# Scaling the samples by a diagonal, left halves first, and a last stage over 128 partitions: one hybrid layer step on one core

## The reference, cut to what matters

```python
def trunk(x, ...):
    h = rmsnorm(x, norm1_g)
    u_s5, x_rg, g_rg, q, k, v, o, gi, gf = split(h @ w_in)
    y1 = s5_mixer(u_s5, ...)      # step = exp(log_step); mag = exp(lr*step); cos, sin(li*step); complex scan
    y2 = rglru_mixer(x_rg, ...)   # causal conv of 4, two sigmoids, scan
    y3 = mlstm_mixer(q, k, v, gi, gf, o, ...)
    x = x + concat(y1, y2, y3) @ w_out
    x = x + moe(rmsnorm(x, norm2_g), ...)   # 32 experts: w1 1024x2048, w2 1024x1024
    return rmsnorm(x, final_norm_g)         # x / sqrt(mean(x*x) + eps) * g
```

## Time and profile before

| | us |
|---|---|
| median of 3 runs (lowest, highest) | 1098.44 (1097.82, 1098.92) |
| the profiled execution | 1098.81 |
| its span, first to last instruction | 1097.0 |
| PE busy | 1036.5 (94%) |
| DVE busy | 316.1 (29%) |
| ACT busy | 197.9 (18%) |
| POOL busy | 95.3 (9%) |
| moved | 429.45 MB, 391 GB/s over the span |
| chain that ended last | PE 55%, DMA 36%, DVE 5%, ACT 2% |

### The profile page before, as it was taken

How to read it: one execution, slowest core, us unless ns; L and a number is a source line. 1 busy time by engine, 2 the same in 40 slices (tenths; PEclk the granted TensorE clock), 3 DMA queues, 4 the chain that set the end, 5 groups by cost and what they waited for, 6 DMA issues and landing times.

```text
span 1097.0 us, 13183 instructions
## 1 busy us (share of the span) xinstructions
PE 1036.5 (94%) x5134; PEld 435.2 (40%) x5134; DVE 316.1 (29%) x640; ACT 197.9 (18%) x418; POOL 95.3 (9%) x177
## 2 busy tenths in 40 slices
PE   8999999999999999899889989999899989998997
PEld 5767745334333433343333323333324233433322
DVE  5889456312131212121202112121212121212023
ACT  5543615401110201011000201020102010100002
POOL 6899000000000000000000000000000000000000
PEclk9999999999999999999999999999999999999999
DMA  7533799999999999999999999999999999999995
GB/s 223 194 114 77 260 370 406 427 426 431 430 433 430 430 431 431 431 431 431 434 431 431 431 431 431 431 431 434 431 430 431 431 431 431 431 433 431 424 426 239
DMA packets 62051, 429.45 MB, mean 391 GB/s; under 512 B 12022, under 2 KB 25054, under 8 KB 33342
## 3 DMA queue, kind: packets, MB, share of 16 engines
q1 hardware_dynamic: 60868, 428.16, 93.5%
q10 hardware_dynamic: 1146, 0.79, 0.2%
HBM read 424.68 MB, written 3.67 MB: 390 GB/s over the span
## 4 chain that ended last, share of the span: by engine, by line
PE 55%; DMA 36%; DVE 5%; ACT 2%; issue 1%; SPq 1%; ACTq 0%; DVEq 0%
DMA ring_a<-in_exp_w_dram 27%; PE psum L2405 17%; PE psum L2440 14%; DMA ring_b<-in_exp_w_dram 8%; PE psum L2426 7%; PE psum L2327 3%; PE psum L2158 3%; PE psum L2350 2%; PE psum L1886 2%; PE psum L2449 1%; PE psum L2277 1%; PE psum L2283 1%; DVE rgb L1341 1%; SPq L449 1%; DMA xn<-in_x_prompt_dram 1%
## 5 line engine op out<-in xcount | busy, mean ns | idle before, releaser
L2405 PE MATMUL psum<-ring_a,xg 128*64 128x512 f32 x1200 | 341.8, 600 | 14.4 <-DMA ring_a<-in_exp_w_dram 14.4
L2440 PE MATMUL psum<-ring_a,aT 128*64 128x512 f32 x768 | 217.7, 596 | 8.5 <-DMA ring_a<-in_exp_w_dram 8.2
L2405 PEld LDWEIGHTS psum<-ring_a,xg 128*64 128x64 f32 x1200 | 102.9, 137 | 170.1 <-issue 166.0
L2405 PE MATMUL psum<-ring_b,xg 128*64 128x512 f32 x368 | 152.3, 598 | 7.8 <-DMA ring_a<-in_exp_w_dram 7.8
L1672 DVE TENSOR_TENSOR x<-x,psum 128x512 f32<-128x512 f32 x60 | 41.2, 687 | 367.7 <-PE psum L2350 367.7
L2426 PE MATMUL psum<-ring_a,xg 128*64 128x512 f32 x336 | 103.5, 608 | 14.2 <-DMA ring_b<-in_exp_w_dram 14.2
L2440 PEld LDWEIGHTS psum<-ring_a,aT 128*64 128x64 f32 x768 | 68.0, 137 | 110.2 <-issue 104.3
L2440 PE MATMUL psum<-ring_b,aT 128*64 128x512 f32 x256 | 104.0, 595 | 4.2 <-DMA ring_a<-in_exp_w_dram 2.6
L1760 DVE TENSOR_SCALAR acts<-psum 128x512 f32<-128x512 f32 x32 | 22.0, 688 | 223.3 <-PE psum L2426 207.8
L1045 ACT ACTIVATE acts<-acts 128x512 f32<-128x512 f32 x32 | 20.1, 627 | 296.5 <-DVE acts L1760 296.5
L2405 PEld LDWEIGHTS psum<-ring_b,xg 128*64 128x64 f32 x368 | 43.1, 136 | 75.5 <-issue 63.6
(11 more groups left out here) (508 smaller groups left out, 934.9 us busy)
## 6 DMA issues: line engine op xcount, KB each, us to landing
ring_a<-in_exp_w_dram SPq DMA_DIRECT2D x144, 2048.0 KB, 26.3
ring_b<-in_exp_w_dram SPq DMA_DIRECT2D x46, 2048.0 KB, 24.8
ring_a<-in_w_in_dram SPq DMA_DIRECT2D x4, 2048.0 KB, 8.5
ring_a<-in_w_out_dram SPq DMA_DIRECT2D x2, 2048.0 KB, 9.8
ring_a<-in_w_in_dram SPq DMA_DIRECT2D x3, 1024.0 KB, 5.9
ring_a<-in_state_ml_c_dram SPq DMA_DIRECT2D x4, 512.0 KB, 6.1
out_dram<-ring_a SPq DMA_DIRECT2D x4, 512.0 KB, 6.1
ring_b<-in_exp_w_dram SPq DMA_DIRECT2D x2, 1024.0 KB, 28.5
```

Source lines behind the costliest of these rows:

```text
L2405: m = M(psum[64 * x:64 * x + 64, bk, :], xg[:, k, u, 64 * x:64 * x + 64], w[x][:, 512 * bk:512 * bk + 512], start=False, stop=(k == KD - 1))
L2440: m = M(psum[64 * x:64 * x + 64, 4 + nn, :], aT[:, 2 * j + s, 64 * x:64 * x + 64], w[x][:, 1024 * s + 512 * nn:1024 * s + 512 * nn + 512], ...
```

## The change

Six edits, in the opening and at the end.

1. The samples are not scaled by VectorE over 1024 columns. VectorE scales a 32x32 identity instead (`scale_diag`), and TensorE multiplies the samples' blocks with it in place of transposing them.
2. VectorE takes out hT0, hT2, hT4, hT3, hT5, ScalarE only hT1. TensorE waits for the three left halves ahead of u0 and for the three right halves inside u0, behind its fourth step. Two of the four `keep_warm` products behind the first transposes go.
3. ScalarE takes the magnitude and the RG values behind a signal of its own (`mag_arg`), and waits for `angle_reduced` only ahead of the sines.
4. The five loads for `par` move from SyncE's queue to ScalarE's, with the two bias loads, behind the sines; `glw` moves behind `w_in1`. TensorE turns `par` inside xr0, behind its sixth step; ScalarE copies u1 and gp ahead of `bias_piece(0)` and `par`.
5. At the end the samples lie as four quarters of 256 columns over 128 partitions, in one bank (`END_UNITS`, `end_parts`, `sample_sums`): four residual copies, four narrow products.
6. Their sums of squares (one per partition and quarter) are added by one product with `quarters`, a matrix that VectorE builds (`add_quarters`); root, inverse and the last product follow on 128 partitions with `gf_quarters`, copied from `gfb` in four pieces.

```diff
@@ sync
                 if c == 1:
...
-                    for x, name in enumerate(("state_s5_re", "state_s5_im")):
-                        sp.dma_start(srow[64 * x:64 * x + 64, :], ...).then_inc(sem("par_loaded"), 16)
-                    sp.dma_start(prow[0:32, :], ...).then_inc(sem("par_loaded"), 16)
-                    sp.dma_start(prow[32:48, :], ...).then_inc(sem("par_loaded"), 16)
-                    sp.dma_start(prow[48:96, :], ...).then_inc(sem("par_loaded"), 16)
...
+                if c == 2:
                     sp.dma_start(glw[:], ...).then_inc(sem("glw_loaded"), 16)
-                if c == 2:
...
-                sp.dma_start(o[1].rearrange("b t n -> (b t) n"), y_out[0:TS, 2, :]).then_inc(sem("stored"), 16)
+                sp.dma_start(o[1].rearrange("b t (w n) -> w (b t) n", w=4), y_out[:, 2, 0:256]).then_inc(sem("stored"), 16)
@@ scalar
-            for i in range(2):
-                name = f"hT{2 * i + 1}"
...
-            act.dma_start(bias_in[:, 0:512], ...).then_inc(sem("bias_loaded"), 16)
-            act.dma_start(bias_in[:, 512:768], ...).then_inc(sem("bias_loaded"), 16)
+            await_fill(act, "hT1")
+            for c in range(4):
+                m = A(hT[:, 4 + c, 0:128], bank("hT1")[:, 128 * c:128 * c + 128], ACT.Copy, scale=vec("norm1_g", 4 + c))
+            m.then_inc(drained[FILLS["hT1"][0]], 1)

             A(sm[:, 1, :], vecs[:, NVEC:NVEC + J5], ACT.Exp).then_inc(says_now("step_ready"), 1)
-            act.wait_ge(*at("angle_reduced", 1))
+            act.wait_ge(sem("mag_arg"), 1)
             A(sm[:, 5, :], sm[:, 2, :], ACT.Exp).then_inc(says_now("mag_ready"), 1)
...
+            act.wait_ge(*at("angle_reduced", 1))
             A(sm[:, 6, :], sm[:, 9, :], ACT.Sin).then_inc(says_now("angle_ready"), 1)
             A(sm[:, 7, :], sm[:, 8, :], ACT.Sin).then_inc(says_now("angle_ready"), 1)
+            act.dma_start(bias_in[:, 0:512], ...).then_inc(sem("bias_loaded"), 16)
+            act.dma_start(bias_in[:, 512:768], ...).then_inc(sem("bias_loaded"), 16)
+            for x, name in enumerate(("state_s5_re", "state_s5_im")):
+                    act.dma_start(srow[64 * x:64 * x + 64, :], ...).then_inc(sem("par_loaded"), 16)
+            act.dma_start(prow[0:32, :], ...).then_inc(sem("par_loaded"), 16)
+            act.dma_start(prow[32:48, :], ...).then_inc(sem("par_loaded"), 16)
+            act.dma_start(prow[48:96, :], ...).then_inc(sem("par_loaded"), 16)
...
             u_out(0)
+            u_out(1)
+            copy_out("gp", gate_parts, bank("gp")[:, 0:T])
             bias_piece(0)
-            u_out(1)
             copy_out("par", parT[:, 0:224], bank("par")[:, 0:224])
-            copy_out("gp", gate_parts, bank("gp")[:, 0:T])
...
+                A(psum[:, 4, 0:256], sample_sums, ACT.Square, accum_out=st2[:, 2:3]).then_inc(sem("ms3_ready"), 1)
+                act.wait_ge(sem("quarters_added"), n // 3 + 1)
+                A(st2[:, 6:7], psum[:, 3, 0:1], ACT.Sqrt, scale=1.0 / D, bias=st2[:, 12:13]).then_inc(sem("root3_ready"), 1)
@@ vector
+                    says(TSC(scale_diag, ident[0:n, 0:n], nst[0:n, 4 + i:5 + i], None, ALU.mult), "xn_ready", i + 1)
...
-            for k in (0, 2, 4, 5):
+            for k in (0, 2, 4, 3, 5):
...
+                V.tensor_reduce(gts[:, 0, :], ident[:].rearrange("p (w t) -> p t w", w=4), AX.X, ALU.add).then_inc(sem("quarter_made"), 1)
+                dve.wait_ge(sem("quarter_made"), r + 1)
+                V.tensor_copy(quarters.rearrange("p (w t) -> p w t", w=4), ...).then_inc(sem("quarters_ready"), 1)
...
                 dve.wait_ge(sem("gf_loaded"), 16)
+                for w in range(4):
+                    q = slice(TS * w, TS * w + TS)
+                    dv(V.tensor_copy(gf_quarters[q], gfb[q, 256 * w:256 * w + 256]))
...
+                        STT(out=y_out[:, i, 0:256], in0=sample_sums, scalar=st2[:, 4 + i:5 + i], in1=gf_quarters,
+                            op0=ALU.mult, op1=ALU.mult).then_inc(sem("y_final"), 1)
@@ tensor
+                        m = M(bank(f"hT{k}")[:, 128 * c:128 * c + n], rows_, scale_diag, start=True, stop=True)
...
-                if k == 3:
-                    keep_warm(1)
-            keep_warm(2)
+            keep_warm(1)
...
+            rows_turned(0)
             pe.wait_ge(sem("w_in0"), 16)
-            channels("u0", 0, 0)
+            channels("u0", 0, 0, lambda k: rows_turned(1) if k == 3 else None)
             channels("u1", 0, 128)
...
-            channels("xr0", 0, 256)
+            channels("xr0", 0, 256, state_rows)
...
+                    for w in range(4):
+                        m = M(psum[n * w:n * w + n, END_BANKS[c], 0:256], sgt[:, t0:t0 + n], ..., start=False, stop=True)
...
+            def add_quarters(n, r):
+                pe.wait_ge(sem("ms3_ready"), n + 3)
+                pe.wait_ge(sem("quarters_ready"), r + 1)
+                M(psum[:, 3, 0:1], quarters, st2[:, 2:3], start=True, stop=True).then_inc(sem("quarters_added"), 1)
```

113 lines of the change are left out of this document (69 added, 44 removed).

## The result

| | before | after |
|---|---|---|
| median of 5 runs (lowest, highest), us | 1098.71 (1097.82, 1098.92) | 1105.43 (1103.27, 1106.43) |
| the profiled execution | 1098.81 | 1105.43 |
| its span | 1097.0 | 1103.7 |

A forecast was written before the change was run, and what follows sets the result against it. The expert-weight stream, set by the DMA engines, bounds the middle, so only its start and what follows it can gain: 1.05 + 0.6 = 1.65 us off 1098.44 gives 1096.8 us, range 1095.7 to 1098.3.

The forecast's parts named there:

- Step 1: Opening: VectorE's sample product shrinks from 32x1024 (0.80 us) to 32x32, taken as 0.20, so first hT product starts at 10.43.
- Step 2: Opening: TensorE's first projection u0 needs only left halves, starts at 12.50 us, 0.9 us early; two fewer warming products cost nothing.
- Step 3: Opening: sines run at 15.55 us, VectorE goes on at 16.0 instead of 18.34, 2.3 us early; GpSimd's tables as well.
- Step 4: Opening: moved loads shut ScalarE's sequencer from 15.6 to 19.5 but land in time; VectorE's 2.3 us lead shrinks to 1.5.
- rival B: Opening pays nothing: a 1 us stall between 16 and 45 us eats the 1.05; 1097.8 us, chance 0.18.
- Rival C: Opening: parameters land late beside `w_in1`, TensorE stands in xr0 until 27.4; kernel slower at 1099.7 us, chance 0.10.
- Step 5: At the sigmoids, where TensorE's and the other engines' trains meet, the smaller gain counts: weight stream starts 1.05 us early.
- Steps 6 and 7: End: added residual and opening work is hidden; narrower combining issues the sample store at 1093.0 instead of 1094.08, 1.1 early.
- Step 8: End: the sample store queues behind two prompt stores, so of the 1.1 us 0.6 arrives, between 0.3 and 1.1.

The follow-up runs named there:

- f3: The kernel before with the new end alone, opening untouched: 1099.34 us beside 1098.75, ratio 0.9998.
- h4: The kernel before with the new end alone, its samples' store split as four transfers over two queues: 1099.86 us beside 1098.97, ratio 1.0008.
- g2: The kernel before with the early sines (`mag_arg`) alone, no load moved: 1102.05 us beside 1099.05, ratio 1.003.
- e1: The changed kernel with the five parameter loads back on SyncE ahead of `w_in1`: 1105.13 us beside 1099.09, ratio 1.0043.
- g1: e1 with GpSimd's tables held until ScalarE has copied u0 out: 1099.82 us beside 1099.05, ratio 0.9999.
- g3: The kernel before with the moved queues, new copy order and moved parameter transposes alone, sines late: 1107.35 us beside 1099.05, ratio 1.0076.
- h1: The changed kernel, loads late as they are, with GpSimd's tables held until ScalarE has copied u0 out: 1107.8 us beside 1098.97, ratio 1.0079.
- f4: e1 with VectorE's 128x384 product ahead of the scans in the last four S5 rounds: 1102.91 us beside 1098.75, ratio 1.0035.
- e3: The changed kernel with SyncE issuing `w_in1` only when parameter and bias loads have landed: 1104.18 us beside 1099.09, ratio 1.0035.
- e4: The changed kernel with the samples' store as four transfers of 32 rows instead of one: 1105.74 us beside 1099.09, ratio 1.0057.
- f1: e1 with the two bias loads between ScalarE's first two exponentials, ahead of the sines: 1106.85 us beside 1098.75, ratio 1.0059.
- f2: The changed kernel with 14 warming products on TensorE in xr0 ahead of the wait for the parameters: 1107.2 us beside 1098.75, ratio 1.007.
- e2: The changed kernel with the parameter loads ahead of the bias loads, both on ScalarE's queue: 1109.77 us beside 1099.09, ratio 1.0103.

## Why the prediction was wrong, step by step

**Step 1, the samples' scale.** 0.44 us instead of 0.20, an instruction over 32 elements; the sum had 0.6 and won 0.36. Small.

**Step 2, left halves first.** Right for u0: 12.01 (12.50 forecast; the first transposes of x start 0.66 us earlier in this execution). "Two warming products fall away ... no cost" rests on a clock that I took as given: it fell to 0.50 at 12.4 us, 1.6 us lost. This is no property of the change alone. Of 14 profiles with the new opening five show it, of six with the old opening two (f3, h4). I had read one execution of the kernel before, which did not have it.

**Step 3, the early sines.** The table load ahead of its wait was right (13.50 to 14.78, the sine at 15.16), the sines came at 15.16 (15.55 forecast). The draining that the Trainium skill, page "ScalarE: Activation LUTs", section "What ACT_TABLE_LOAD costs", adds to each switch was not seen: the sine starts 0.38 us behind the load. The step that failed is three words, "GpSimd's tables as well", booked as a gain. GpSimd's tables are 53 us of work (18.27 to 71.24 before), beside which VectorE's instructions are stretched. With GpSimd started at 15.29 and nothing else changed but VectorE's own earlier way, the kernel is 3 us slower (g2), and GpSimd held back restores the time (e1 against g1).

Over all 20 profiles VectorE's busy time goes with how far GpSimd is ahead of it, from GpSimd's first table instruction to the point where VectorE goes on. This is a relation read from traces; g1 and g3, which move one of the two each, agree with it. With a lead of 6.6 to 8.8 us VectorE is busy for 29.1 to 30.3 us on its way to the RG scan in eight of ten profiles, and for 31.4 and 32.4 in two (h1, h4). With 9.0 to 9.6 us (e1, f4, g2) it is 32.3 to 32.6, with 11.0 to 14.2 us (the change, e3, e4, f1, f2, g3) 35.8 to 36.8, and with 18.0 us (e2) 34.3. In the changed kernel the lead is 14.2 us instead of 8.6; 2.7 of the 5.6 come from the early sines (step 3) and 2.8 from the late loads (step 4).

**Step 4, the moved DMAs.** Here the main loss lies. The issue times were right (the sequencer shut from 15.2 to 20.3, forecast 15.6 to 19.5). The landing times were not: `bias_piece(0)` at 23.2 and the transposes at 24.5 presume loads that land in 3 to 4 us; the kernel before had 1.8 to 2.5. They took 7.0 to 8.9. Their place behind two bias loads and `w_in1` beside them make some 4 us each when alone, and 7.1 together (e2, e3). `w_in1` was issued at 16.1 and not at 17.9; the turns between queues, on which the forecast counted, did not bring the loads in on time. The bias loads were late too; that VectorE would stand for them had been in rival B, at 1 us, and it was 4.90.

**Rival C was the mechanism, mis-sized.** It named the stall in xr0, and its threshold, 28.4; the parameters landed at 28.73. By its own sum a landing at 28.73 gives about 1101.0 us (an estimate: 2.5 us past the 26.2 at which it becomes slower); 1105.43 was measured. Its price left out three things: 3.4 us for the clock behind the stall, VectorE's way beside GpSimd (33.9 us before, 39.65 after), and the end. The first two lie on trains that run side by side and do not add. It got 0.10 since "four of the five loads start before `w_in1` moves"; in the trace none did (16.48 and later; `w_in1` was issued at 16.11). The trace of before had no row of a small load behind a slow one on the same queue, and that unknown should have been a bound of the range, not an argument.

**Step 5, where the trains meet.** The rule "the smaller gain counts" assumes that each train keeps its pace. Neither does. In e1 both trains were early, 1.1 and 1.7 us, and nine of twelve runs were 5 us late or more. In six profiles TensorE idled 2.34 to 4.10 us at its first S5 products behind 70 us, the clock fell, and the rounds behind took 6.2 us (e1, e2, e3, f1, g2, h4). In the eleven others with the old order of products that wait is 0.34 to 1.80 us, and no round did. The changed kernel is one of the eleven: its loss is the one of steps 3 and 4, not this one.

**Steps 6 and 7, the end's work.** Right: hidden, and 1.21 us earlier at the store (1.1).

**Step 8, who is late next.** Right that the gain would not arrive, wrong that 0.6 would: the end is 0.9 us longer in the profile (0.5 to 1.0 over the others). The store was costed by its bytes; its form had changed as well, and its last packet ends 0.8 us later behind the combining, though it is issued 1.21 earlier.

The chances: 0.05 for slower by over 0.2%, which is what happened.

## What to carry to other kernels

A load that is moved behind others on a queue can land with them: cost it from the landing of the slowest load ahead of it and from what other queues move then, not from its own size. Work of GpSimd beside VectorE is not free cover; starting it earlier, or VectorE later, is a change to VectorE's time, and it can turn a gain into a loss. Where several engines are within a microsecond of each other, price the stall that you see and what it sets off: an idle TensorE, a clock at half, the next engine late.

## What was not expected of the hardware

- VectorE instructions of 0.17 to 0.21 us took 0.90 to 1.12 where they began inside a GpSimd product of 1.1 to 1.3 us. With a GpSimd product started 0.03 us ahead a VectorE product took 1.79 us instead of 0.69 to 0.85, four times in a row.
- The same 78 VectorE instructions were busy for 29.1 to 36.8 us, and the time went with how far GpSimd's work was ahead of them.
- A wait of 2.94 us of TensorE was followed by 7 us at a granted clock of 0.50, so it cost 6.3 us; 14 products without use in its place did not prevent that.
- The same kernel took 1098 us three times and 1105 us nine times (e1), and with one wait of GpSimd all runs lay between 1098.1 and 1100.7 (g1).
- 24 KB took 8.9 us from issue to landing. 128 KB stored as four quarters in rows of 1 KB made the end 0.5 to 1 us longer than in rows of 4 KB, whether as one transfer or as four, but with one the data were late and with four what follows them.
